# A decoder layer on one core: the input projection is fed with x before its norm, and the norm's row factor is applied to the result

## The reference, cut to what matters

```python
h = rms_norm(x, norm_g[0])               # x * rsqrt(mean(x*x) + eps) * g
p = h @ w_in + b_in                      # 60 column blocks of 128, and 8 narrow columns
y_A, y_B, y_C = gating(p), gated_delta_rule(p), stick_breaking_attention(p)
m = sum_i sigmoid(gate_i(p)) * (y_i @ w_branch_i)
x = x + rms_norm(m @ w_out, norm_g[1])
f = square(relu(rms_norm(x, norm_g[2]) @ w_ff1)) @ w_ff2
out = x + rms_norm(f, norm_g[3])
```

## Time and profile before

| | |
|---|---|
| median of 3 runs | 2322.13 us |
| the profiled execution | 2324.92 us |
| its span, first to last instruction | 2323.1 us |
| mean granted TensorE clock, of full speed | 0.955 |
| busy: PE, DVE, ACT, POOL | 91%, 39%, 35%, 5% |
| opening, until the products run without gaps | 0 to 51.5 us |
| phase 1, attention, delta rule | to 190, to 634, to 1172 us |
| spatial gating, branches, output and norms | to 1298, to 1446, to 1596 us |
| feed-forward, last norm | to 2292, to 2323 us |

### The profile page before, as it was taken

How to read it: one execution, slowest core, us unless ns; L and a number is a source line. 1 busy time by engine, 2 the same in 40 slices (tenths; PEclk the granted TensorE clock), 3 DMA queues, 4 the chain that set the end, 5 groups by cost and what they waited for, 6 DMA issues and landing times.

```text
span 2323.1 us, 26938 instructions
## 1 busy us (share of the span) xinstructions
PE 2112.4 (91%) x9786; PEld 1639.2 (71%) x9786; DVE 906.6 (39%) x1229; ACT 814.1 (35%) x1297; POOL 126.6 (5%) x79
## 2 busy tenths in 40 slices
PE   6998888888999999999979899977999999999994
PEld 3885555555678787877747688845888888888883
DVE  4113535354462534436223556245322322322335
ACT  4224646565633534334223433233301302302311
POOL 2000000000012030302100000022000000000002
PEclk7998999898999999999989999987999999999997
DMA  3222111212121212112042443311111111111113
GB/s 119 101 81 82 42 68 41 72 44 72 67 103 37 99 36 92 61 54 72 18 190 90 182 136 120 134 74 44 45 54 45 45 54 45 45 54 45 45 45 145
DMA packets 51530, 174.16 MB, mean 75 GB/s; under 512 B 5536, under 2 KB 5536, under 8 KB 51488
## 3 DMA queue, kind: packets, MB, share of 16 engines
q1 hardware_dynamic: 50336, 171.52, 20.7%
q10 hardware_dynamic: 1152, 2.10, 0.2%
HBM read 127.45 MB, written 46.14 MB: 75 GB/s over the span
## 4 chain that ended last, share of the span: by engine, by line
PE 67%; DVE 8%; ACT 5%; DMA 4%; issue 4%; SPq 1%; POOL 1%; ACTq 0%; DVEq 0%; POOLq 0%
PE gemm L306 16%; PE gemm L308 16%; PE gemm L307 16%; DMA w_raw<-w_stream 2%; PE dn L1091 2%; PE dn L1089 2%; PE gemm L1170 2%; PE gemm L1171 1%; PE gemm L1172 1%; PE attn_out L1021 1%; ACT w_hi L294 1%; DVE d_cv L1306 1%; PE z L992 1%; DMA a_k<-projections 1%; DVE a_sp_lo L1263 1%
## 5 line engine op out<-in xcount | busy, mean ns | idle before, releaser
L306 PE MATMUL gemm<-act_hi,w_hi 128*128 128x512 f32 x1600 | 667.1, 417 | 40.4 <-DVE act_lo L469 16.2
L308 PE MATMUL gemm<-act_hi,w_lo 128*128 128x512 f32 x1600 | 636.5, 398 | 0.0
L307 PE MATMUL gemm<-act_lo,w_hi 128*128 128x512 f32 x1600 | 636.2, 398 | 0.0
L306 PEld LDWEIGHTS gemm<-act_hi,w_hi 128*128 128x128 f32 x1600 | 307.5, 192 | 125.1 <-issue 36.7
L308 PEld LDWEIGHTS gemm<-act_hi,w_lo 128*128 128x128 f32 x1600 | 307.5, 192 | 67.5
L298 DVE TENSOR_TENSOR w_lo<-w_raw,w_hi 128x1024 fp32r<-128x1024 f32 x144 | 177.5, 1233 | 452.5 <-ACT w_hi L294 447.7
L307 PEld LDWEIGHTS gemm<-act_lo,w_hi 128*128 128x128 f32 x1600 | 308.8, 193 | 61.6 <-issue 6.5
L294 ACT ACTIVATE w_hi<-w_raw 128x1024 fp32r<-128x1024 f32 x144 | 151.4, 1052 | 334.6 <-PE gemm L308 281.5
L332 ACT ACTIVATE stage<-gemm,cols 128x512 f32<-128x512 f32 x120 | 82.2, 686 | 338.1 <-PE gemm L308 332.6
L306 PE MATMUL gemm<-f_hi,w_hi 128*128 128x512 f32 x512 | 199.2, 389 | 0.0
L307 PE MATMUL gemm<-f_lo,w_hi 128*128 128x512 f32 x512 | 199.2, 389 | 0.0
(11 more groups left out here) (225 smaller groups left out, 2506.3 us busy)
## 6 DMA issues: line engine op xcount, KB each, us to landing
w_raw<-w_stream SPq DMA_DIRECT2D x144, 512.0 KB, 3.5
projections<-stage SPq DMA_DIRECT2D x60, 512.0 KB, 2.9
gate<-projections SPq DMA_DIRECT2D x48, 256.0 KB, 2.8
d_in<-projections SPq DMA_DIRECT2D x12, 512.0 KB, 4.5
y_lo<-branch_outputs SPq DMA_DIRECT2D x6, 1024.0 KB, 12.0
x_sb<-xT SPq DMA_DIRECT2D x4, 1024.0 KB, 8.6
x_fin<-xT SPq DMA_DIRECT2D x4, 1024.0 KB, 8.0
residual<-mixed SPq DMA_DIRECT2D x8, 512.0 KB, 2.6
```

What stands on the lines that cost most here:

```text
L306: nc.tensor.matmul(g_bank[hf][:], w_hi[s][:, k, :], a_hi[:, k, t], start=(k == 0), stop=False)
L307: nc.tensor.matmul(g_bank[hf][:], w_hi[s][:, k, :], a_lo[:, k, t], start=False, stop=False)
L308: last = nc.tensor.matmul(g_bank[hf][:], w_lo[s][:, k, :], a_hi[:, k, t], start=False, stop=(k == KT - 1))
```

## The change: what it does

The projection's activations become x times gain, without the row factor: ACT writes `act_hi` straight from x (Copy with the gain as scale), DVE writes `act_lo` as x times gain minus `act_hi`. Squares are added on DVE into `sum0`, and one float32 matmul with ones for each half gives the sums. x arrives in eight transfers, four for each token half; the gains come ahead of it. The first weight pair has buffers of its own and both its blocks are computed together, k by k, in the banks `gemm0`, `gemm1`, `z0`, `z1`, first all of token half 0, then half 1; the second pair's weights are loaded and split meanwhile.

Every half of a projection block, all 120, is now multiplied by `rstd0` on DVE on its way from PSUM to `stage` (`scale_projection`), which raises `bank_read`; ACT then adds the bias and applies the function in place in `stage`, which raises `staged`, and SP stores after that. The same holds in the slots of phases 2 to 4. In the norm ahead of the feed-forward DVE makes all eight lower parts and POOL none. `g_rstd` now shares memory with `g_mean`. The counters of the norm semaphores are renumbered. The diff, cut to its core:

```diff
+            sum0 = sb("sum0", [P, S])
+            f_raw = [sb(f"f_raw{s}", [P, KT * P]) for s in range(2)]
+            fw_hi = [sb(f"fw_hi{s}", [P, KT, P], f32r) for s in range(2)]
+            fw_lo = [sb(f"fw_lo{s}", [P, KT, P], f32r) for s in range(2)]
...
+        def split_hi(act, n, s, first=False, free=False):
             act.wait_ge(raw_loaded[s], 16 * n + 16)
-            if not first:
+            if not (first or free):
                 act.wait_ge(blk_done[s], n)
-            nc.scalar.activation(w_hi[s][:], w_raw[s][:].rearrange("p (k c) -> p k c", k=KT), ACT.Copy).then_inc(hi_ready[s], 1)
-
-        def split_lo(dve, n, s):
+            raw, hi = (f_raw, fw_hi) if first else (w_raw, w_hi)
+            nc.scalar.activation(hi[s][:], raw[s][:].rearrange("p (k c) -> p k c", k=KT), ACT.Copy).then_inc(hi_ready[s], 1)
+        def split_lo(dve, n, s, first=False):
             dve.wait_ge(hi_ready[s], n + 1)
-            nc.vector.tensor_tensor(w_lo[s][:], w_raw[s][:].rearrange("p (k c) -> p k c", k=KT),
-                                    w_hi[s][:].bitcast(f32), ALU.subtract).then_inc(lo_ready[s], 1)
+            raw, hi, lo = (f_raw, fw_hi, fw_lo) if first else (w_raw, w_hi, w_lo)
+            nc.vector.tensor_tensor(lo[s][:], raw[s][:].rearrange("p (k c) -> p k c", k=KT),
+                                    hi[s][:].bitcast(f32), ALU.subtract).then_inc(lo_ready[s], 1)
...
+        def scale_projection(dve, n, s, hf, src=None):
+            wait_half(dve, n, s, hf, 2 * n + s)
+            if hf == 0:
+                dve.wait_ge(stored[s], 1 + 16 * n)
+            settle(dve)
+            t = slice(HALF * hf, HALF * hf + HALF)
+            nc.vector.tensor_tensor(stage[s][:, t], g_bank[hf][:], rstd0[:, t], ALU.mult).then_inc(bank_read[hf], 1)
         def take_projection(act, n, s, hf, func):
-            wait_half(act, n, s, hf, 2 * n + s)
-            if hf == 0:
-                act.wait_ge(stored[s], 1 + 16 * n)
+            act.wait_ge(bank_read[hf], 1 + 2 * n + s + 1)
             settle(act)
-            nc.scalar.activation(stage[s][:, HALF * hf:HALF * hf + HALF], g_bank[hf][:], func,
-                                 bias=cols[:, ds(V_BIN + 2 * n + s, 1)]).then_inc(bank_read[hf], 1)
+            t = slice(HALF * hf, HALF * hf + HALF)
+            nc.scalar.activation(stage[s][:, t], stage[s][:, t], func, bias=cols[:, ds(V_BIN + 2 * n + s, 1)]).then_inc(staged[s], 1)
         def store_projection(sp, n, s):
-            sp.wait_ge(bank_read[0], 1 + 2 * n + s + 1)
-            sp.wait_ge(bank_read[1], 1 + 2 * n + s + 1)
+            sp.wait_ge(staged[s], 2 * n + 2)
             sp.dma_start(pT[2 * n + s], stage[s][:]).then_inc(stored[s], 16)
...
         def dve_beside(dve, b):
             for step in b.steps():
                 blk, r = divmod(step, 16)
+                n, s = b.n0 + blk // 2, blk % 2
+                if r == 7:
+                    scale_projection(dve, n, s, 0)
                 if r == 15:
-                    split_lo(dve, b.n0 + blk // 2 + 1, blk % 2)
-
-
-        def norm_squares(act, i, src, buf, ready, after=lambda k: None):
+                    scale_projection(dve, n, s, 1)
+                    split_lo(dve, n + 1, s)
...
-        def normalised(dve, i, src, gain, rstd, buf):
+        def normalised(dve, src, gain, rstd, buf):
             for k in range(KT + 1):
                 if k < KT:
                     if k >= 4:
-                        dve.wait_ge(hl_ready[k % 2], 4 * min(i, 1) + k // 2 - 1)
+                        dve.wait_ge(hl_ready[k % 2], k // 2 - 1)
                     nc.vector.scalar_tensor_tensor(buf[k % 4][:], src[:, k, :], cols[:, gain + k:gain + k + 1], rstd[:],
                                                    ALU.mult, ALU.mult).then_inc(h_ready, 1)
-                if k % 2:
-                    lower_part(nc.vector, i, k - 1, buf)
+                if k:
+                    lower_part(nc.vector, k - 1, buf)
...
-            for r in range(4):
-                sp.dma_start(x_sb[:, 2 * r:2 * r + 2, :], xT[2 * r:2 * r + 2].rearrange("k p s -> p k s")).then_inc(x_in[r], 16)
-                if r in (1, 2):
...
-            sp.dma_start(cols[:], cols_in).then_inc(cols_loaded, 16)
-            sp.dma_start(wbd[:], w_bd).then_inc(loaded, 16)
-            sp.dma_start(consts[:], consts_in).then_inc(loaded, 16)
-
+            sp.dma_start(cols[:, 0:V_LNG], cols_in[:, 0:V_LNG]).then_inc(g_loaded, 16)
+            for r in range(8):
+                hf, q = divmod(r, 4)
+                t = slice(HALF * hf, HALF * hf + HALF)
+                sp.dma_start(x_sb[:, 2 * q:2 * q + 2, t], xT[2 * q:2 * q + 2, :, t].rearrange("k p s -> p k s")).then_inc(x_in[r], 16)
+                if r in (0, 1):
+                    load_weights(sp, 0, r, first=True)
...
+            sp.dma_start(cols[:, V_LNG:], cols_in[:, V_LNG:]).then_inc(cols_loaded, 16)
+            for s in range(2):
+                load_weights(sp, 1, s)
+            sp.dma_start(wbd[:], w_bd).then_inc(loaded, 16)
+            sp.dma_start(consts[:], consts_in).then_inc(loaded, 16)
+            for s in range(2):
+                store_projection(sp, 0, s)
+            with sp.Fori(1, N_SB) as i:
                 for s in range(2):
                     sp_block(sp, i, s)
...
             exp_ln_tables()
-            norm_squares(act, 0, lambda k: x_sb[:, k, :], sq0, ready=lambda k: (x_in[k // 2], 16),
-                         after=lambda k: split_hi(act, 0, k - 4, first=True) if k in (4, 5) else None)
-            act.wait_ge(ones_set, 2)
-            norm_root(act, 0, rstd0)
-            for k in range(KT):
-                act.wait_ge(h_ready, k + 1)
-                nc.scalar.activation(act_hi[:, k, :], hbuf[k % 4][:], ACT.Copy).then_inc(hh_ready, 1)
+            act.wait_ge(g_loaded, 16)
+            def root0(hf):
+                t = slice(HALF * hf, HALF * hf + HALF)
+                act.wait_ge(x_ss, hf + 1)
+                nc.scalar.activation(rstd0[:, t], d_bank[hf][:], ACT.Ln, scale=1.0 / D, bias=eps).then_inc(x_ln, 1)
+                act.wait_ge(x_ln, hf + 1)
+                nc.scalar.activation(rstd0[:, t], rstd0[:, t], ACT.Exp, scale=-0.5).then_inc(x_root, 1)
+            for hf in range(2):
+                t = slice(HALF * hf, HALF * hf + HALF)
+                for k in range(KT):
+                    act.wait_ge(x_in[4 * hf + k // 2], 16)
+                    nc.scalar.activation(act_hi[:, k, t], x_sb[:, k, t], ACT.Copy, scale=cols[:, V_NORM + k:V_NORM + k + 1]).then_inc(x_hi, 1)
+                    if k == 0:
+                        nc.scalar.activation(sum0[:, t], x_sb[:, k, t], ACT.Square).then_inc(x_sq, 1)
+                    else:
+                        c = 7 * hf + k - 1
+                        if c >= 3:
+                            act.wait_ge(x_sum, c - 2)
+                        nc.scalar.activation(sq0[c % 3][:], x_sb[:, k, t], ACT.Square).then_inc(x_sq, 1)
+                    if hf == 0 and k in (1, 2):
+                        split_hi(act, 0, k - 1, first=True)
+                    if hf and k == 2:
+                        act.wait_ge(ones_set, 2)
+                        root0(0)
+                    if hf and k in (4, 5):
+                        split_hi(act, 1, k - 4, free=True)
+            root0(1)
             act.wait_ge(loaded, 32)
             nc.scalar.activation(wbd_parts[:], ident[:, None, :].broadcast_to([P, KT, P]), ACT.Copy, scale=0.0).then_inc(wbd_zero, 1)
             act.wait_ge(wbd_zero, 1)
             nc.scalar.activation(wbd_parts[:, :, 0:8], wbd[:], ACT.Copy).then_inc(small, 1)
-            with act.Fori(0, N_SB - 1) as i:
+            for hf in range(2):
+                for s in range(2):
+                    take_projection(act, 0, s, hf, ACT.Identity)
+            with act.Fori(1, N_SB - 1) as i:
                 for s in range(2):
                     act_block(act, i, s, ACT.Identity)
...
-            norm_products(pe, 0, sq0)
-            pe.wait_ge(loaded, 32)
+            def sum0_product(hf):
+                t = slice(HALF * hf, HALF * hf + HALF)
+                pe.wait_ge(x_sum, 7 * hf + 7)
+                nc.tensor.matmul(d_bank[hf][:], ones[:], sum0[:, t], start=True, stop=True).then_inc(x_ss, 1)
+            first_banks = (g_bank, z_bank)
             for hf in range(2):
-                product_half(pe, 0, 0, hf, act_hi, act_lo, 0, ready=lambda k: (hl_ready[k % 2], k // 2 + 1))
-            pe_block(pe, 0, 1, act_hi, act_lo, 0)
-            with pe.Fori(1, N_SB - 2) as i:
+                pe.wait_ge(bank_read[hf], 1)
+                t = slice(HALF * hf, HALF * hf + HALF)
+                for k in range(KT):
+                    pe.wait_ge(x_lo, KT * hf + k + 1)
+                    for s in range(2):
+                        if hf == 0 and k == 0:
+                            pe.wait_ge(lo_ready[s], 1)
+                        o = first_banks[s][hf][:]
```

(61 more changed lines are left out.)

70 lines of the change are left out of this document (33 added, 37 removed).

## The result

The changed kernel takes 2387.90 us (median of 4 runs, 2385.62 to 2394.76), the kernel before, run beside it, 2322.09. The ratio is 1.0283, with a 95% interval of 1.0256 to 1.0309. The profiled execution has a span of 2384.8 us against 2323.1, 61.7 more.

The account below looks back on a forecast made before the run. PE was taken as busy 91% of the span, the rest waiting, with an ACT-DVE-ACT-DVE-PE chain setting attention's pace. 54.3 us lost against 30.4 gained made 23.9 slower: 2346 us against the median 2322.13, range 2315 to 2361.

Parts of the forecast that it names:

- The opening: Start of kernel: nothing waits for the row factor, pair 1 starts at 41.9 instead of 68.91, minus 27.0 us.
- The norm: Ahead of the feed-forward: lower parts on DVE alone take 19.5 us instead of 22.9, minus 3.4 us (bounds 2 and 5).
- The cost of an evacuation: Each half taken from PSUM: DVE product, hand-over and in-place ACT operation make ACT's next work 0.7 us later.
- Attention: Attention heads: 0.7 us at 20 takes already followed by PE waits, and at four head ends, 16.8 us lost.
- Clock: Attention heads: a wait grown from 3.32 to 4.0 us may drop TensorE's clock, 4.8 us lost (bounds 0 and 10).
- rival C: Clock drops in every attention head and at each delta-rule start: 12 us more, 2358 us; chance 0.07.
- Delta rule, the rest of a head: Delta-rule takes after the head's start: four times 0.7 us plus 0.7 for two more, 14.0 us lost in four heads.
- The head start: Delta-rule head starts: DVE scales the first half only behind the conv of q, 15.2 us lost in four heads.
- The rest: Spatial gating, 0.7 us at three places, and ends of phases 1 and 4, 0.7 each: 3.5 us lost.
- Rival A: Slack inside the heads takes up the added 0.7 us; only delta-rule starts and head and phase ends cost: 2312.5 us; chance 0.14.
- B: Rival: no change, about 2322 us, opening as computed and half of the added waits passing through; chance 0.11.
- D: Rival: opening's supply runs as before, PE at lower clock through the first pair, 10 us less gain, 2356 us; chance 0.05.

Follow-up runs that it names:

- Experiment 2: Changed kernel with ScalarE's split of the next weights ahead of its take of a block's last half, phases 2 to 4: 2331.30 us (ratio 1.0043).
- experiment 4: Changed kernel, ScalarE taking only last halves, or only first halves, straight from PSUM behind phase 1, without their row factor: 2332.83 and 2365.32 us.
- Experiment 3: Changed kernel, VectorE's delta-rule slot 1 scaling issued ahead of the convolutions: 2401.43 us; also with ScalarE's weight split ahead of the last-half take: 2337.05 us.

## Why the prediction was wrong

The direction held, and the sum of the gains nearly (30.4 forecast, 27.2 measured). The loss was 89 us in the three stages, forecast at 54.3 with the phase ends, so the time lies above the range. By term, in us; waits are length minus PE busy, clock is the growth of PE's busy time:

| term | forecast | measured |
|---|---|---|
| opening and phase 1 | -27.0 | -22.8 |
| branches, output, norms | -3.4 | -4.4 |
| attention, waits | 16.8 | 18.7 |
| delta rule, head start, waits | 15.2 | 11.1 |
| delta rule, rest of a head, waits | 14.0 | 29.4 |
| the rest: gating and phase ends (measured: gating), waits | 3.5 | 6.2 |
| clock, in the three stages | 4.8 | 23.3 |

Two steps failed: the delta rule's "rest of a head", short by 15.4 us, and the clock, short by 18.5.

**The opening** was put at -27.0. Pair 1 starts at 43.47, forecast 41.9, against 68.91 in the earlier trace rows:

```profile
6.84 0.72 ACT L698 ACTIVATE act_hi<-x_sb,cols 128x512 fp32r<-128x512 f32 x1 [4.82 <-DMA x_sb<-xT]
11.57 0.77 PE L1002 MATMUL gemm<-act_hi,fw_hi 128*128 128x512 f32 x1 [11.57 <-DVE fw_lo L307]
33.98 0.50 PE L1002 MATMUL gemm<-act_hi,fw_hi 128*128 128x512 f32 x1 [2.90 <-DVE act_lo L1282]
43.47 0.50 PE L315 MATMUL gemm<-act_hi,w_hi 128*128 128x512 f32 x1
```

The stall for the row factor is 2.90, as worked out. ACT's first operation on x came at 6.84 and not at 4.9, later than the 5.86 of the earlier trace rows though with half the bytes. That is -25.4, and 2.6 are given back up to attention: 0.8 at the border of the phases, put at 0.7, and 1.8 in matmuls at the lower level (granted clock 0.97 in place of 0.99 over phase 1). "Phase 1: nothing" thus missed by 1.8. **The norm**, -3.4: from the first product (1638.43) to the end of the last lower part (1657.27) it is 18.8 us, forecast 19.5, before 22.9. The first squares come 4.0 us earlier.

**The cost of an evacuation**, 0.7: measured 0.88 at the takes in the chain, at 3.32 to 4.20 as at 1.15 to 2.04. The step "an ACT operation in SBUF of 625 ns" took the duration of an operation without a column operand; with it, 722. So ACT gains nothing against its 686 from PSUM.

**Attention**, 16.8: five takes by four heads by 0.88 are 17.6, the waits grew by 18.7 in all. The mechanism and the places were right. The forecast of 114 us a head came out at 115.6.

**Clock**, 4.8, with bounds 0 and 10: 8.3 in attention, 11.5 in the delta rule, 3.5 in the gating. The step that failed is "after the 3.32 us wait it stayed up", which was read from the second head alone. In the first head of the kernel before it did not:

```profile
254.19 0.44 PE L1002 MATMUL dn<-a_sp_hi,a_from 128*128 128x384 f32 x1 [3.32 <-DVE a_sp_lo L1263]
255.98 0.63 PE L308 MATMUL gemm<-act_hi,w_lo 128*128 128x512 f32 x1
```

The one head was also the argument against the second half of rival C. Rival C, held at 0.07, named the clock, with 12 us more than the forecast. It came at the starts of all four heads of the delta rule, behind waits of 8.09 and three times 3.81 us (before: at one start, behind 3.87), and also, which C had not, behind four of the waits of 2.4 us (at 980.48, 1061.30, 1126.53 and 1207.59), which had been 1.5 us or nothing. By the rule of the Trainium skill ("TensorE: Matmul & The Clock Gate", section on HAM oscillation) waits that recur in a loop can drop the clock each time. The traces agree in part: the clock fell behind the wait of 4.20 us in all four heads, behind 3.32 in one of four and behind 2.71 in two of four, and nearly the same waits in three runs of the same attention code gave PE 382.3, 390.0 and 391.9 us busy.

**Delta rule, the rest of a head**, 14.0: 29.4. This is the step that failed by its mechanism. The two takes before the scan's and the last sums' matmuls, and the one before L1162 (then L1091), grew by 3.5 each, as put (0.7 x 4, at 0.88). But "0.7 for two takes at places nearly without slack" hid 9.8 us at L1152 and 7.3 at L1148. The error is in a sentence of the part on the cost of an evacuation: that at r = 15 "the same 0.7 falls" before `split_lo`. It holds only where ACT and DVE reach the slot together. Where DVE comes later, the chain was DVE alone; it became DVE, ACT, ACT, DVE, and cost 0.69 + 1.83 = 2.5, by the timeline at 832.96 (a PE wait of 2.5 where there was none). Experiment 2 shows it for L1152: started without DVE, the split takes 7.7 us of these 9.8 away, and experiment 4 removes them with the last halves. For L1148 it does not: the order takes away 1.7 of 7.8. There the first halves take part, and how is open.

**The head start**, 15.2: PE waits 13.5 us more for the bank, of which the second head's 3.81 was forecast at 2.4 more than nothing, and 2.4 less for the inverse norm, together 11.1. The wait was there as forecast, and its sum was put too high. Experiment 3, which moves slots 1, 2 and 3, shows that the wait is then handed on, since the convolutions are as close to the chain as the bank.

**The rest**, 3.5: 6.2 of waits in the gating alone. I counted three takes there, and the waits grew by 2.4 us for `g_sq`, 3.8 for `g_n` and 0.9 for `g_v`. The order of experiment 2 gives 5.6 of the stage's 9.7 us back; which of these waits are due to the round trip was not taken apart.

**Rival A** falls (the wait behind the take went from 1.15 to 2.04), and so do B (the waits passed through) and D (the opening did what it says).

## What to carry to other kernels

A step handed to a second engine costs more than its duration: wherever the second engine's program already waits for the first, the hand-over closes a loop, and both stand in it. Before moving an operation, write down for each place which engine arrives first; then put what the other waits for ahead of the new hand-over. And a factor that can be applied once to the operand, in a stage with slack, beats one that is applied at every result. Last, read a wait and the clock behind it in every turn of a loop: one turn is not the others.
